# Second block's attention: the division of the probabilities moved from VectorE to GpSimd

## The chip, the cores and the metric

The kernel runs on one core of one Trainium2 chip. The metric is the device time of one execution in microseconds (us). One core has five engines, each with its own instruction stream: TensorE (PE in the profile, with PEld for its weight loads), VectorE (DVE), ScalarE (ACT), GpSimd (POOL) and SyncE (SP), which here issues the weight transfers. Engines wait for each other by semaphores only.

## What is computed

Two transformer-like blocks of two layers each over 256 tokens of width 1024, all in 32-bit floats. The first block is not touched. Of the second block each layer is attention with 16 softmax maps and then 16 experts of which each picks 32 tokens:

```
s = jnp.einsum(...).astype(jnp.float32) * scale          # 256 x 256 per head
s = s + bias        # 4 neighbourhood heads; 6 latent heads have no bias; 6 window heads have a mask and a sink logit
p = jax.nn.softmax(s, axis=-1).astype(v.dtype)
o = einsum(p, v)
h = h + concat(rms_norm(o_a), rms_norm(o_b), rms_norm(o_c)) @ w_out[l]
h = h + expert_choice_ffn(rms_norm(h, ffn_norm[l]), w_router[l], w_gate[l], w_up[l], w_down[l])
```

## The kernel before

Every engine's program is written out by hand in one order, and no scheduler changes it. In the second block the order of the attention part of a layer is the list `window_order(l)`: all engines walk the same list, and each executes of a step what is its own. I call this stretch of a layer "the window"; in the profile it lies at about 1060 to 1122 us (layer 0) and 1636 to 1700 us (layer 1). A map is called a unit, numbered 0 to 15: units 0 to 3 have a bias, 4 to 9 are the latent heads, 10 to 15 have the mask and the sink. A unit s goes through these steps:

- `s_qk` (TensorE): the scores, 128x512 (128 queries a partition, two halves of them, 256 keys each) into a PSUM bank.
- `m_max` (VectorE): adds the bias where there is one (L1654), takes the maximum (L1662), with the sink a maximum with it, and writes its negative (L1650, 128x2), signal `nmax`.
- `e_exp` (ScalarE): two exponentials 128x256 with their sums (L2443), with the sink one more of 128x2; signal `exp2`. It writes one of four buffers `sc2[2 + s % 4]`, and so waits for the transposes of unit s - 4.
- `n_norm` (VectorE): for sink units adds the sink's term to the sums (L1646, 128x2), the reciprocal of the sums (L1666, 128x2), and two multiplications in place, one for each half of 128x256 (L1650); signal `scaled2`.
- `t_turn` (TensorE): four transposes (L707, for units 0 to 3 L711), `c_copy` (ScalarE) their copy from PSUM (L2447), `v_pv` (TensorE) the product with the values for a pair of units, `w_out` (ScalarE) its square and its scaled copy, `q_stat` (TensorE) sums of the squares, `o_w` (TensorE) the output projection of a group of heads, `y_x` (VectorE, L1654 into x) its addition to the residual.

The three output groups g have a root each (`r_root`): VectorE sums (L1662) and scales (L1650), GpSimd raises to the power -1/2 (L2968), and VectorE waits for that. Before the window, `l_mkv` copies and `l_rot` rotates on VectorE. Some steps have idle matmuls put ahead of them (`SPARE`), which fill a wait of TensorE.

The experts' weights are fetched by SP in one fixed queue. The first of them for a layer go into room that the window frees: blocks "combine" wait for `v_pv` 4, "rest" for `s_qk` 15, "more" for `t_turn` 15, the next ones for `v_pv` 7 and one for the router. Every engine's helpers have `own()`, a wait for the engine's own last instruction. GpSimd's whole program in the second block before the change is the roots.

Of the kernel before, what the change touches and what calls it, by code (L numbers as in the profile page):

```python
# [17 lines left out]
def const_arrays():  # L18
# [65 lines left out]
    "merge": "gate gate_t bra brb mA gated merged gt1 gt1_dg gt2 gt2_dg",  # L84
    "hidden": "relu relu2 h1_hi h1",
    "latent": "lat_sq latent cro nab aqk cqT mq mkv mq_rot acT mT",
    "attn2": "s2 biased nmax exp2 scaled2 pT2 pv2 sq2 oT2",
    "group": "stat g_sum xg",
    "route": "router logits aff_e aff affT chosen sel slot Pm0 Pm xn xs0 xs1 PA PW x_apart",
    "norm": "root normed",  # L90
# [210 lines left out]
def program(nc, a, c1off, c2off, out):  # L301
    ctx = ExitStack()
    with ctx:
# [397 lines left out]
        def tensor(e):  # L701
# [697 lines left out]
                    psum.until(psum.at["s2", l, s], A, "exp2", l, s)  # L1399

            def t_turn(l, s):
                e.wait_ge(*V("scaled2", l, s))
                k, pb = bank("pT2", l, s)
                e3 = v4(sc2[2 + s % 4], 2)
                for t in range(2):
                    for kt in range(2):
                        turn_ = tr_flipped if s < 4 else tr
                        m = turn_(pb[:, 256 * t + 128 * kt:256 * t + 128 * kt + 128], e3[:, t, 128 * kt:128 * kt + 128])
                m.then_inc(*P.up("pT2", l, s))
# [228 lines left out]
        def vector(e):  # L1638
# [29 lines left out]
            def step():  # L1668
                return V.up("step")
# [631 lines left out]
            def n_norm(l, s):  # L2301
                u, st = units[s], S(f"u{s}", 10)
                e.wait_ge(*A("exp2", l, s))
                if u["sink"] is not None:
                    tt(st[:, 4:6], st[:, 4:6], st[:, 8:10], ALU.add).then_inc(*step())
                reciprocal(st[:, 6:8], st[:, 4:6]).then_inc(*step())
                e3 = v4(sc2[2 + s % 4], 2)
                for t in range(2):
                    m = ts(e3[:, t, :], e3[:, t, :], st[:, 6 + t:7 + t], None, ALU.mult)
                    m.then_inc(*(V.up("scaled2", l, s) if t else step()))  # L2310

            def r_root(l, g):
                c0, nc = groups[g]
# [645 lines left out]
        def pool(e):  # L2959

            def own():
                if G.last is not None:
                    e.wait_ge(*G.last)

            def root(v, *key):
                e.wait_ge(*V("root", *key))
                own()
                e.tensor_tensor(v, v, bc(K("nhalf"), [128, v.shape[1]]), ALU.pow).then_inc(*G.up("root", *key))  # L2968

            def levels(l):  # L2970
                e.wait_ge(*V("LT", l, 1))
                for s in range(1, 6):
                    for i in range(2):
                        if s > 1:
                            e.wait_ge(*P("B", l, s - 1, i))
                        a8, l8 = (z[:, i].rearrange("p t h c -> p (t h) c") for z in (AT, LT))
                        own()
                        e.tensor_tensor(a8, l8, bc(K(("lvF" if i == 0 else "lvB") + str(s)).unsqueeze(1), [128, 8, 64]),
                                        ALU.mult).then_inc(*G.up("AT", l, s, i))

            root(rstd[:, :], "x0", 0)
            for l in range(2):
                root(S("ya_ss", 8), "ya", l)
                levels(l)
                root(S("yb_ss", 8), "yb", l)
                root(rstd[:, :], "out", l)
                root(rstd[:, :], "mlp", l)
            for l in range(2):
                root(S("lat", 4), "lat", l)
                for g in range(3):  # L2990
                    root(S(f"gss{g}", 2), "g", l, g)
                root(rstd[:, :], "out2", l)
                if l == 0:
                    root(rstd[:, :], "moe", l)
            for t in range(2):
                root(rstd[:, t:t + 1], "last", t)
# [107 lines left out]
```

## Time and profile before

| | |
|---|---|
| median of 3 runs | 2171.55 us (2168.85 to 2175.55) |
| the profiled execution's own time, its span | 2170.66 us, 2169.4 us |
| busy: PE, DVE, ACT, POOL | 1861.0, 905.7, 643.6, 43.2 us |
| DMA, mean over the span | 285 GB/s |
| window of layer 0, 1060 to 1122 us: PE, DVE, ACT, POOL busy | 58.12, 51.51, 37.06, 1.39 us |
| window of layer 1, 1636 to 1698 us: the same | 54.27, 51.39, 37.24, 1.39 us |

A row of a timeline has its start, its length, the engine, the line, the operation, output <- input, and in brackets the idle time of the engine before it with what ended that. Rows of one kind that follow each other are merged (x8 is eight instructions). A multiplication of four passes stands as several MATMUL rows. Matmul lengths are modelled at their ends, so two rows may overlap a little. `ar`, `small`, `c`, `ring`, `x` are memory areas of the program, `pb` a PSUM bank.

### The profile page before, as it was taken

The page shows a single profiled execution, that of the slowest core. Times are in us where ns is not written, and L with a number is a line of the kernel's source. Part 1 is how long each engine was busy: PE and PEld are TensorE (multiplying, and loading weights), DVE is VectorE, ACT ScalarE, POOL GpSimd, SP SyncE. Part 2 cuts the span into 40 slices and gives each one's busy share as a digit, 9 for nine tenths or more (in the row PEclk, how much of TensorE's full clock was granted, in tenths as well). Part 3 has the DMA queues.
Part 4 walks back from the last instruction along what each step waited for, and adds up shares of the span by engine and source line. Part 5 has one row for each costly group of instructions (what it writes and reads, how often), then busy time and mean ns, then how long its engine had stood idle before and what let it go on. Part 6 is the DMA issues. An engine that isn't in the chain of part 4 may idle for free.

```text
span 2169.4 us, 31018 instructions
## 1 busy us (share of the span) xinstructions
PE 1861.0 (86%) x12840; PEld 1233.1 (57%) x12840; DVE 905.7 (42%) x1506; ACT 643.6 (30%) x1110; POOL 43.2 (2%) x46
## 2 busy tenths in 40 slices
PE   6999999999999999999898866676798997666666
PEld 3887888987888888988754311121275542121212
DVE  3675585655576576645762200000058520000002
ACT  3244235545244235534452100000055410000001
POOL 0001000000001000000000000000000000000000
PEclk8999999999999999999999987888899998888888
DMA  9565348456634344553749999999984799999997
GB/s 339 217 233 195 118 155 311 178 184 221 233 117 157 118 156 157 193 194 83 258 193 374 428 426 428 426 428 426 422 264 160 310 408 427 426 427 427 427 425 315
DMA packets 119749, 617.45 MB, mean 285 GB/s; under 512 B 18448, under 2 KB 21434, under 8 KB 86586
## 3 DMA queue, kind: packets, MB, share of 16 engines
q1 hardware_dynamic: 119034, 613.85, 71.6%
q8 instruction: 102, 1.67, 0.3%
q10 hardware_dynamic: 576, 1.63, 0.2%
q14 instruction: 37, 0.30, 0.0%
HBM read 614.40 MB, written 1.05 MB: 284 GB/s over the span
## 4 chain that ended last, share of the span: by engine, by line
PE 59%; DMA 27%; DVE 9%; ACT 2%; issue 1%; SPq 0%; POOL 0%; DVEq 0%; ACTq 0%
PE pb L704 57%; DMA ring<-in_w_up_dram 18%; DMA ar<-in_w_up_dram 4%; DMA x<-in_w_up_dram 3%; PE pb L707 2%; DVE ar L1654 2%; DVE ar L1646 1%; ACT ar L2443 1%; DMA ring<-in_ada_w_dram 1%; DMA ring<-in_w_down_dram 1%; DVE ar L1650 1%; DVE small L1662 1%; DVE x L1646 1%; ACT ar L2447 0%; DVE ar L1658 0%
## 5 line engine op out<-in xcount | busy, mean ns | idle before, releaser
L704 PE MATMUL pb<-ring,ar 128*32 128x512 f32 (+2 forms) x2144 | 408.5, 731 | 183.1 <-DMA ring<-in_w_up_dram 102.5
L704 PE MATMUL pb<-ar 64*64 64x64 f32 (+10 forms) x3680 | 418.9, 348 | 37.8 <-DMA ring<-in_w_up_dram 30.8
L2447 ACT COPY ar<-pb 128x512 f32<-128x512 f32 (+2 forms) x195 | 112.7, 578 | 910.1 <-PE pb L704 852.3
L1658 DVE COPY ar<-pb 128x512 f32<-128x512 f32 (+3 forms) x94 | 57.5, 612 | 723.2 <-PE pb L704 713.5
L704 PEld LDWEIGHTS pb<-ring,ar 128*32 128x32 f32 (+1 forms) x2144 | 106.4, 133 | 397.0 <-issue 383.0
L704 PEld LDWEIGHTS pb<-ar 64*64 64x64 f32 (+5 forms) x3680 | 217.9, 146 | 188.9 <-issue 165.9
L704 PE MATMUL pb<-hT,ring 128*128 128x256 f32 x1024 | 235.4, 386 | 0.4 <-ACT ar L2443 0.4
L704 PEld LDWEIGHTS pb<-hT,ring 128*128 128x128 f32 x1024 | 193.0, 192 | 33.6 <-issue 7.8
L1646 DVE TENSOR_TENSOR ws<-ring,ws 128x1024 fp32r<-128x1024 f32 x128 | 156.9, 1226 | 123.8 <-ACT ws L2447 122.0
L704 PE MATMUL pb<-hs,ws 128*128 128x256 f32 x1536 | 186.0, 283 | 3.7 <-ACT aux L2447 1.5
L704 PEld LDWEIGHTS pb<-hs,ws 128*128 128x128 f32 x1536 | 184.7, 192 | 5.6 <-ACT aux L2447 1.7
L704 PE MATMUL pb<-ws,h1s 128*128 128x512 f32 x768 | 175.7, 390 | 0.0
L2447 ACT CAST ws<-ring 128x1024 fp32r<-128x1024 f32 x128 | 134.2, 1048 | 127.2 <-PE pb L704 123.4
L704 PEld LDWEIGHTS pb<-ws,h1s 128*128 128x128 f32 x768 | 144.0, 188 | 30.8 <-issue 1.0
L704 PE MATMUL pb<-wp,hp 128*128 128x512 f32 (+1 forms) x636 | 140.0, 380 | 3.3 <-DVE wp L1646 1.6
L704 PEld LDWEIGHTS pb<-wp,hp 128*128 128x128 f32 x636 | 114.7, 190 | 27.3 <-DVE wp L1646 3.9
L707 PE MATMUL pb<-c,ar 128*128 128x128 f32 (+3 forms) x580 | 85.8, 283 | 23.8 <-DMA c<-in_c_dram 9.2
L707 PEld LDWEIGHTS pb<-c,ar 128*128 128x128 f32 (+3 forms) x580 | 68.7, 155 | 65.9 <-issue 39.9
L704 PE MATMUL pb<-hT,ar 128*32 128x512 f32 x200 | 67.2, 805 | 34.3 <-DMA ring<-in_w_up_dram 34.3
L1646 DVE TENSOR_TENSOR wp<-ring,wp 128x1024 fp32r<-128x1024 f32 (+1 forms) x53 | 61.2, 1155 | 55.9 <-ACT wp L2447 54.4
L2447 ACT CAST wp<-ring 128x1024 fp32r<-128x1024 f32 (+1 forms) x53 | 52.6, 992 | 56.0 <-PE pb L704 54.9
L1654 DVE SCALAR_TENSOR_TENSOR ar<-ar,pb 128x256 f32<-128x256 f32 (+1 forms) x84 | 40.7, 485 | 64.8 <-ACT ar L2443 57.7
(177 smaller groups left out, 1647.8 us busy)
## 6 DMA issues: line engine op xcount, KB each, us to landing
ring<-in_w_down_dram SPq DMA_DIRECT2D x46, 2048.0 KB, 28.1
ring<-in_w_gate_dram SPq DMA_DIRECT2D x42, 2048.0 KB, 28.4
ring<-in_w_up_dram SPq DMA_DIRECT2D x42, 2048.0 KB, 23.6
ring<-in_w_mlp_dram SPq DMA_DIRECT2D x32, 2048.0 KB, 7.9
ring<-in_w_in_dram SPq DMA_DIRECT2D x27, 2048.0 KB, 9.2
ring<-in_ada_w_dram SPq DMA_DIRECT2D x24, 2048.0 KB, 8.0
ar<-in_w_gate_dram SPq DMA_DIRECT2D x12, 2048.0 KB, 27.7
ar<-in_w_up_dram SPq DMA_DIRECT2D x12, 2048.0 KB, 23.5
```

The source lines that it names most:

```text
L704: return e.matmul(o, l, r, start=start, stop=stop)
L707: return e.transpose(o, i, ident[0:i.shape[0], 0:i.shape[0]])
L1646: return e.tensor_tensor(o, i0, i1, op)
L1650: return e.tensor_scalar(o, i, s1, s2, op0, op1)
L1654: return e.scalar_tensor_tensor(out=o, in0=i0, scalar=s, in1=i1, op0=op0, op1=op1)
L1658: return e.tensor_copy(o, i)
L1662: return e.tensor_reduce(o, i, AX.X, op)
L2443: return e.activation(o, i, fn, scale=scale, **kw)
L2447: return e.copy(o, i)
```

## The change

Of `n_norm` VectorE keeps the sink's addition and the reciprocal, whose signal is now `whole2`. The two multiplications of 128x256 go to GpSimd, which waits for `whole2` and, ahead of each, for its own last instruction; TensorE's `t_turn` now waits for GpSimd's signal. GpSimd walks `window_order` for these and for the three roots, so a root now stands behind the divisions that the list has ahead of it.

```diff
--- before.py
+++ after.py
@@ -84,7 +84,7 @@
     "merge": "gate gate_t bra brb mA gated merged gt1 gt1_dg gt2 gt2_dg",
     "hidden": "relu relu2 h1_hi h1",
     "latent": "lat_sq latent cro nab aqk cqT mq mkv mq_rot acT mT",
-    "attn2": "s2 biased nmax exp2 scaled2 pT2 pv2 sq2 oT2",
+    "attn2": "s2 biased nmax exp2 whole2 scaled2 pT2 pv2 sq2 oT2",
     "group": "stat g_sum xg",
     "route": "router logits aff_e aff affT chosen sel slot Pm0 Pm xn xs0 xs1 PA PW x_apart",
     "norm": "root normed",
@@ -1399,7 +1399,7 @@
                     psum.until(psum.at["s2", l, s], A, "exp2", l, s)
 
             def t_turn(l, s):
-                e.wait_ge(*V("scaled2", l, s))
+                e.wait_ge(*G("scaled2", l, s))
                 k, pb = bank("pT2", l, s)
                 e3 = v4(sc2[2 + s % 4], 2)
                 for t in range(2):
@@ -2303,11 +2303,7 @@
                 e.wait_ge(*A("exp2", l, s))
                 if u["sink"] is not None:
                     tt(st[:, 4:6], st[:, 4:6], st[:, 8:10], ALU.add).then_inc(*step())
-                reciprocal(st[:, 6:8], st[:, 4:6]).then_inc(*step())
-                e3 = v4(sc2[2 + s % 4], 2)
-                for t in range(2):
-                    m = ts(e3[:, t, :], e3[:, t, :], st[:, 6 + t:7 + t], None, ALU.mult)
-                    m.then_inc(*(V.up("scaled2", l, s) if t else step()))
+                reciprocal(st[:, 6:8], st[:, 4:6]).then_inc(*V.up("whole2", l, s))
 
             def r_root(l, g):
                 c0, nc = groups[g]
@@ -2978,6 +2974,17 @@
                         e.tensor_tensor(a8, l8, bc(K(("lvF" if i == 0 else "lvB") + str(s)).unsqueeze(1), [128, 8, 64]),
                                         ALU.mult).then_inc(*G.up("AT", l, s, i))
 
+            def n_norm(l, s):
+                e3 = v4(sc2[2 + s % 4], 2)
+                e.wait_ge(*V("whole2", l, s))
+                for t in range(2):
+                    own()
+                    m = e.tensor_scalar(e3[:, t, :], e3[:, t, :], S(f"u{s}", 10)[:, 6 + t:7 + t], None, ALU.mult)
+                    m.then_inc(*(G.up("scaled2", l, s) if t else G.up("step")))
+
+            def r_root(l, g):
+                root(S(f"gss{g}", 2), "g", l, g)
+
             root(rstd[:, :], "x0", 0)
             for l in range(2):
                 root(S("ya_ss", 8), "ya", l)
@@ -2987,8 +2994,9 @@
                 root(rstd[:, :], "mlp", l)
             for l in range(2):
                 root(S("lat", 4), "lat", l)
-                for g in range(3):
-                    root(S(f"gss{g}", 2), "g", l, g)
+                for step_, *key in window_order(l):
+                    if step_ in ("n_norm", "r_root"):
+                        (n_norm if step_ == "n_norm" else r_root)(l, *key)
                 root(rstd[:, :], "out2", l)
                 if l == 0:
                     root(rstd[:, :], "moe", l)
```

The order of VectorE's instructions changes in 16 places of each layer in the same way. The first piece is VectorE in layer 0, from the division of unit 2 to that of unit 6, with the maximum of unit 7 between (`pb6` and so on are the PSUM banks). Before:

```order
L1666 RECIPROCAL small<-small 128x2
L1650 TENSOR_SCALAR ar<-ar,small 128x256 x2
L1666 RECIPROCAL small<-small 128x2
L1650 TENSOR_SCALAR ar<-ar,small 128x256 x2
L1666 RECIPROCAL small<-small 128x2
L1650 TENSOR_SCALAR ar<-ar,small 128x256 x2
L1662 TENSOR_REDUCE small<-pb6 128x2
L1650 TENSOR_SCALAR small<-small 128x2
L1666 RECIPROCAL small<-small 128x2
L1650 TENSOR_SCALAR ar<-ar,small 128x256 x2
```

And now, the same stretch and the maxima of units 8 and 9 behind it:

```order
L1666 RECIPROCAL small<-small 128x2 x3
L1662 TENSOR_REDUCE small<-pb6 128x2
L1650 TENSOR_SCALAR small<-small 128x2
L1666 RECIPROCAL small<-small 128x2 x2
L1662 TENSOR_REDUCE small<-pb7 128x2
L1650 TENSOR_SCALAR small<-small 128x2
L1662 TENSOR_REDUCE small<-pb1 128x2
L1650 TENSOR_SCALAR small<-small 128x2
```

What moved: the multiplications are gone, and the maxima stand directly behind the reciprocals. The second piece is VectorE at the end of layer 0's window: the divisions of units 13 and 14, an addition to x, the maximum of unit 15, another addition to x, the division of unit 15. Before:

```order
L1650 TENSOR_SCALAR ar<-ar,small 128x256 x2
L1654 SCALAR_TENSOR_TENSOR x<-pb0,small,x 128x512
L1654 SCALAR_TENSOR_TENSOR ar<-pb2,ar 128x512
L1662 TENSOR_REDUCE small<-ar 128x2
L1650 TENSOR_SCALAR small<-small,sinks 128x2
L1650 TENSOR_SCALAR small<-small 128x2
L1654 SCALAR_TENSOR_TENSOR x<-pb3,small,x 128x512
L1646 TENSOR_TENSOR small<-small 128x2
L1666 RECIPROCAL small<-small 128x2
L1650 TENSOR_SCALAR ar<-ar,small 128x256 x2
```

And now:

```order
L1646 TENSOR_TENSOR small<-small 128x2
L1666 RECIPROCAL small<-small 128x2
L1654 SCALAR_TENSOR_TENSOR x<-pb0,small,x 128x512
L1654 SCALAR_TENSOR_TENSOR ar<-pb2,ar 128x512
L1662 TENSOR_REDUCE small<-ar 128x2
L1650 TENSOR_SCALAR small<-small,sinks 128x2
L1650 TENSOR_SCALAR small<-small 128x2
L1654 SCALAR_TENSOR_TENSOR x<-pb3,small,x 128x512
L1646 TENSOR_TENSOR small<-small 128x2
L1666 RECIPROCAL small<-small 128x2
```

Here too only the multiplications went. The third piece is GpSimd in one layer of the second block, from the latent part's root to the root of the last group. Before:

```order
L2968 TENSOR_TENSOR small<-small,c 128x4
L2968 TENSOR_TENSOR small<-small,c 128x2 x3
L2968 TENSOR_TENSOR rstd<-rstd,c 128x2 x2
```

And now:

```order
L2964 TENSOR_TENSOR small<-small,c 128x4
L2982 TENSOR_SCALAR ar<-ar,small 128x256 x16
L2964 TENSOR_TENSOR small<-small,c 128x2
L2982 TENSOR_SCALAR ar<-ar,small 128x256 x10
L2964 TENSOR_TENSOR small<-small,c 128x2
L2982 TENSOR_SCALAR ar<-ar,small 128x256 x6
L2964 TENSOR_TENSOR small<-small,c 128x2
L2964 TENSOR_TENSOR rstd<-rstd,c 128x2 x2
```

The divisions of units 0 to 7 stand ahead of the first group's root, those of 8 to 12 ahead of the second's, those of 13 to 15 ahead of the third's.

## Rows read from the trace of the kernel before

**Rows 1.** The page's second part: DMA share and rate in 40 slices.
```profile
DMA  9565348456634344553749999999984799999997
GB/s 339 217 233 195 118 155 311 178 184 221 233 117 157 118 156 157 193 194 83 258 193 374 428 426 428 426 428 426 422 264 160 310 408 427 426 427 427 427 425 315
```
**Rows 2.** The chain that ended last, in order of time: start, length, what.
```profile
1226.70 24.17 DMA ar<-in_w_up_dram
```
**Rows 3.** Busy time in three stretches, both windows and a short one behind.
```profile
1060.00:1122.00 62.00, 58.12 (x298) 38.34 (x298) 51.51 (x138) 37.06 (x100) 1.39 (x2) 0.96 0.44 170
...
1636.00:1698.00 62.00, 54.27 (x286) 34.45 (x284) 51.39 (x136) 37.24 (x103) 1.39 (x2) 1.00 0.44 170
...
1156.00:1160.00 4.00, 4.00 (x38) 1.87 (x31) 1.70 (x2) 0.00 (x0) 0.00 (x0) 1.00 0.25 57
```
**Rows 4.** Timeline of SP, layer 0: two of its issues.
```profile
1122.76 0.33 SPq L3051 DMA_DIRECT2D ar<-in_w_up_dram  x1
...
1158.92 0.33 SPq L3051 DMA_DIRECT2D ring<-in_w_gate_dram  x1
```
**Rows 5.** Groups of VectorE from 1060 to 1122 us, shapes apart.
```profile
L1650 DVE TENSOR_SCALAR ar<-ar,small 128x256 f32<-128x256 f32 x32 | 11.3, 353 | 1.1
...
L1666 DVE RECIPROCAL small<-small 128x2 f32<-128x2 f32 x16 | 2.7, 166 | 1.9 <-POOL small L2968 0.8
```
**Rows 6.** GpSimd: its largest group (ns min/median/max); timeline rows, one of VectorE.
```profile
L2978 POOL TENSOR_TENSOR ar<-ar,c x20: 1090/1092/1601, 199.6 to 712.4; 128x512 f32<-128x512 f32 x20
...
207.33 2.33 POOL L2978 TENSOR_TENSOR ar<-ar,c 128x512 f32<-128x512 f32 x2 [4.68 <-PE pb L704]
...
1094.44 0.17 DVE L1650 TENSOR_SCALAR small<-small 128x2 f32<-128x2 f32 x1
...
1094.69 0.70 POOL L2968 TENSOR_TENSOR small<-small,c 128x2 f32<-128x2 f32 x1 [42.67 <-DVE small L1650]
```
**Rows 7.** Timeline from 199 us, GpSimd and VectorE working at once.
```profile
199.56 3.10 POOL L2978 TENSOR_TENSOR ar<-ar,c 128x512 f32<-128x512 f32 x2 [26.21 <-DVE ar L1646]
200.24 1.46 DVE L1646 TENSOR_TENSOR ar<-c,ar 128x512 f32<-128x512 f32 x1
...
203.24 0.69 DVE L1646 TENSOR_TENSOR ar<-c,ar 128x512 f32<-128x512 f32 x1
```
**Rows 8.** Timeline of TensorE, layer 0: transposes of units 5, 7, 11+12, 13+14, 15.
```profile
1088.09 0.66 PE L707 MATMUL pb<-c,ar 128*128 128x128 f32 x4 [1.15 <-DVE ar L1650]
...
1092.18 0.66 PE L707 MATMUL pb<-c,ar 128*128 128x128 f32 x4 [0.30 <-DVE ar L1650]
...
1108.23 1.40 PE L707 MATMUL pb<-c,ar 128*128 128x128 f32 x8
...
1116.17 1.04 PE L707 MATMUL pb<-c,ar 128*128 128x128 f32 x8
...
1122.08 0.66 PE L707 MATMUL pb<-c,ar 128*128 128x128 f32 x4 [0.83 <-DVE ar L1650]
```
**Rows 9.** Timelines of ScalarE, then VectorE, layer 0.
```profile
1086.48 1.95 ACT L2447 COPY ar<-pb 128x512 f32<-128x512 f32 x3
...
1090.16 0.47 ACT L2443 ACTIVATE ar<-pb,small 128x256 f32<-128x256 f32 x1 [0.46 <-DVE small L1650]
...
1119.29 0.51 ACT L2443 ACTIVATE ar<-ar,small 128x256 f32<-128x256 f32 x1 [1.16 <-DVE small L1650]
...
1121.28 0.74 DVE L1650 TENSOR_SCALAR ar<-ar,small 128x256 f32<-128x256 f32 x2
```
**Rows 10.** Timeline of TensorE, layer 1: units 4, 8, 13 and 14, 15.
```profile
1662.92 0.66 PE L707 MATMUL pb<-c,ar 128*128 128x128 f32 x4 [0.43 <-DVE ar L1650]
...
1675.78 0.66 PE L707 MATMUL pb<-c,ar 128*128 128x128 f32 x4 [0.72 <-DVE ar L1650]
...
1696.27 1.39 PE L707 MATMUL pb<-c,ar 128*128 128x128 f32 x8
...
1698.25 0.66 PE L707 MATMUL pb<-c,ar 128*128 128x128 f32 x4 [0.24 <-DVE ar L1650]
```

## The prediction

> **What bounds the kernel now.** I read four views in this order. First the page's slices: in the experts' part of both layers of the second block the DMA engines move 426 to 428 GB/s without a gap, and between these parts they don't [rows 1]. The chain that ended last says the same: behind 1226 us it is landings of expert weights, some 24 us each, with a few of TensorE's products between them [rows 2]. So the experts' part ends a fixed time after its stream has begun to run without holes, and the window counts through the moment at which it lets the stream go. Then the issues of SP: those that wait for the window are released one by one, "more" at 1122.76 by `t_turn` 15, and after more of TensorE's work one stands at 1158.92, the last before which the DMA engines stood mostly still, with a share of 0.25 from 1156 to 1160 us [rows 3, 4]. From there on nothing waits. A window that ends earlier by d moves all of these by d, and the kernel's end too; each layer pays by itself.
>
> Next, what bounds the window. By busy time VectorE looks like it: 51.5 us of 62, and 12.5 us of that belong to the change. But TensorE is busy for 58.1 us of the 62 in layer 0 and 54.3 in layer 1 [rows 3]. So I looked for the places where TensorE really waits for a division. In layer 0 there are four: 1.15 us at unit 5, 0.30 at unit 7, 0.83 at unit 15, and one hidden in a row: the transposes of units 11 and 12 take 1.40 us for eight, where eight in a row elsewhere take 1.04, so 0.36 of waiting for unit 12 [rows 8]. Together 2.64 us. In layer 1 they are 0.43, 0.72, 0.24 and 1.39 - 1.04 = 0.35, together 1.74 us [rows 10]. What VectorE is freed of elsewhere shortens nothing: TensorE has other work there.
>
> **The change part by part.** Removed from VectorE: per unit two multiplications of 353 ns [rows 5], in a pair 0.74 us [rows 9], with the gap behind it 0.78; 16 units, 12.5 us per layer. The reciprocal of 166 ns stays.
>
> Added to GpSimd: 32 multiplications of 128x256 per layer by a scalar per partition. The trace has none. The nearest row is GpSimd's product of two tensors of 128x512, 1.09 us [rows 6]. With half the elements and one tensor read I take half of it, 0.55 us; below, it can't well beat VectorE's 0.35; above, the full row's 1.09 (all of its cost fixed). Between the two of a pair stands the wait for the own last instruction: two products of 1.09 take 2.33, so 0.15 us of gap [rows 6]. A pair is 1.25 us (0.85 to 2.35). The hand-over from VectorE is small: its instruction ends at 1094.61 and GpSimd's begins at 1094.69, 0.08 us [rows 6]. So a division that follows its exponential at once is ready 0.08 + 1.25 = 1.33 us after the reciprocal instead of 0.76: 0.57 later. One that stood in VectorE's queue is ready earlier.
>
> The Trainium skill, "GPSIMD Engine Reference", section 4.1, says that elementwise work belongs on VectorE, GpSimd being about 2 times slower for two inputs and roughly at line rate for one. By line rate at its 1.2 GHz an instruction would be an estimated 0.21 us and a fixed part, and the gain some tenths larger than below; no run here shows it yet.
>
> Layer 0, in order. Units 0 and 1 have other work of TensorE's ahead of their transposes. Up to 1088.4 us ScalarE works without a pause worth naming (three copies from 1086.48 end it) [rows 9], so the exponentials 3 to 7 don't come earlier whatever VectorE does, and what units 2, 3, 4 gain is not used. Unit 5 is ready about 1.0 us earlier, but the product behind it needs the second of ScalarE's three copies, which ends at 1087.8, and what follows needs the exponential of unit 8, for which ScalarE idles 0.46 us now [rows 9]. That idle goes, and nothing more: of the first two waits (1.45 us) 0.5 comes through. The wait of 0.36 goes wholly, since VectorE then has the maximum of unit 13 and the division of unit 12 done microseconds early. Last the 0.83 at unit 15. Now the exponential of 15 starts at 1119.29 after ScalarE idled 1.16 for its maximum, so its work was done at 1118.13; the multiplications start 2.0 us after it, at 1121.28 [rows 9]. With VectorE ahead it starts as soon as ScalarE is free, at 1118.13 - 0.86 = 1117.3; 2.0 for exponentials, addition and reciprocal and 1.33 for GpSimd give 1120.6. TensorE would be free at 1121.25 - 0.86 = 1120.4, so 0.2 to 0.3 of waiting stays. Layer 0: 0.5 + 0.36 + 0.83 - 0.3 = 1.4 us.
>
> Layer 1. Units 0 and 1 have no cover: their transposes follow their division at once, and come 0.1 and 0.5 us late, of which 0.1 reaches ScalarE's unbroken work behind it. Of the 0.43 at unit 4 the copy ahead of the next product leaves 0.3. Unit 8 waits 0.72 now; its maximum's predecessor comes 0.5 earlier and GpSimd takes 0.57 more, so nothing at that place, but the exponentials behind keep the 0.5. At units 13 to 15 0.35 + 0.24 go, and 0.2 stay as GpSimd's length. With 0.3 for a PSUM bank that unit 15's maximum frees late now: -0.1 + 0.3 + 0.5 + 0.59 - 0.2 + 0.3 - 0.2 (ScalarE) = 1.2 us.
>
> The three roots wait behind divisions that are done by then (the first is wanted at 1094.7, and unit 7's transposes start at 1092.2 [rows 6, 8]): nothing. GpSimd's four buffers, SP's queue and the DMA work stay as they are.
>
> Contention. When GpSimd and VectorE both worked on two tensors in SBUF, VectorE's product took 1.46 us instead of 0.69, and GpSimd's first pair 3.10 instead of 2.33 [rows 6, 7]. In the windows VectorE's long instructions read PSUM or one tensor, and the 128x2 ones are 28 per layer. If each that meets a running multiplication (GpSimd is busy 18 of 60 us) waits half of it, that is 28 x 0.3 x 0.28 = 2.4 us of VectorE per layer, nearly all in time it has just been given: I take 0.1 per layer on the path, 0 to 0.6 as bounds.
>
> The Trainium skill, "SBUF — State Buffer", section "Who interferes with whom", says that VectorE's two-input instructions and its two-port modes (copies and scalar operations from SBUF to SBUF) lock GpSimd out for their whole length, and the other way round. By that rule the trace agrees with the rows of the pair above, and the small scalar operations of `m_max` would be met as well.
>
> Sum: 1.4 + 1.2 - 0.2 = 2.4 us. Against the profiled execution's 2170.66 us (span 2169.4) that gives 2168.3; the median of the runs is 0.9 above that execution, so I say 2169.2. The smallest change that a measurement of this kernel can tell from none is about 0.3%, 6.5 us.
>
> **The rivals.**
> - *GpSimd is the new bound (slower).* In layer 0 the divisions of units 2 to 6 follow each other at the pace of ScalarE's exponentials, about the 1.25 us of a pair. A longer pair queues up: at 2.35 us it falls behind by 1.1 a unit, 5.5 us over five, of which I take 1.4 as covered, 4.1; 1.2 us of waits later in the window go, 1.0 is added at unit 15: +3.9. In layer 1 unit 4 is late by 1.3, +1.5 at the end. Sum +5.4: 2177, still inside 0.3%. It turns from gain to loss at about 0.8 us an instruction, and is slower by over 0.3% from 1.2 us on. At 2 us an instruction GpSimd's 32 would take 66 us, more than a window, and each layer some 12 us: 2195. For it: no row has the operation, its scalar is fetched from memory, and the smallest root takes 0.70 us for 2 elements [rows 6] (it is a power, so I don't price by it). Chance 0.15 for over +6.5 us, 0.15 for a loss within it.
> - *VectorE is the bound after all (faster).* Its rows have no idle time in the windows, and if each wait of ScalarE and TensorE were in the end its fault, all of TensorE's idle time could go: 2.6 us in layer 0, 62 - 54.3 = 7.7 in layer 1, together 10 us, of which GpSimd's latency leaves perhaps 7: 2164.5. Against it: ScalarE's unbroken work [rows 9] and a TensorE that is already nearly full. Chance 0.08 (half of it over 6.5 us).
> - *Blocked ports.* By the mechanism of rows 7 the maxima ahead of units 8 and 15 lose 0.6 each: a gain of 1.2 less, 2170.4. That is the rule of the skill's page named above, were it to apply to the 128x2 instructions. Chance 0.12.
> - *The stream doesn't care.* If the hole at 1158.92 is set by something other than TensorE's order, the windows end earlier and the kernel does not: 2171.5. Against it: that issue waits for TensorE. Chance 0.05.
>
> **How the numbers follow.** My forecast, 1 to 4 us faster, 0.45; the rest as above. Within 0.3%: 0.45 + 0.15 + 0.04 + 0.12 + 0.05 = 0.81, of which I give 0.02 to the faster side for what I may have read too small; faster 0.06, same 0.79, slower 0.15. The range goes down to the rival with 7 us of gain, 2164.5, and up to the bound of GpSimd's price, 2177.5; it leaves out the 0.15 above and a few hundredths below.
>
> **What would show it.** GpSimd's group of 32 x 2 multiplications: at 0.45 to 0.65 us I am right in the price. VectorE's busy time in each window falls from 51.5 to 40. TensorE's waits at units 5, 7, 12 of layer 0 are gone, that at 15 is 0.2 to 0.3 and now put down to GpSimd. SP's issue at 1158.92 comes 1.4 us earlier. VectorE's small instructions beyond 170 ns would show the ports. I am wrong if an instruction of GpSimd takes over 0.8 us, or if TensorE's start of the window's end moves and the last issue does not.

## The result and the profile after

The changed kernel takes 2188.80 us in the median of four runs (2188.32 to 2192.54), the kernel before 2173.09 on the same chip. The ratio is 1.0073, 95% interval [1.0057, 1.0088]: 0.7% slower, about 15.7 us. The forecast was 2169.2, its range ended at 2177.5: the time lies outside it. The profiled execution took 2189.19 us, its span is 2187.8 (before 2169.4), 18.4 us more.

First GpSimd's largest group by line and shape in the changed kernel, over the whole span (busy us, mean ns, idle time before it and what ended it):

```profile
L2982 POOL TENSOR_SCALAR ar<-ar,small 128x256 f32<-128x256 f32 x64 | 59.3, 926 | 79.5 <-DVE small L1666 73.5 <-POOL ar L2982 2.2 <-DVE small L1650 0.7
```

An instruction takes 926 ns, not 550. GpSimd's timeline in layer 0, where the divisions of units 2 to 7 come one after another:

```profile
1083.63 1.94 POOL L2982 TENSOR_SCALAR ar<-ar,small 128x256 f32<-128x256 f32 x2 [4.22 <-DVE small L1666]
...
1087.85 1.94 POOL L2982 TENSOR_SCALAR ar<-ar,small 128x256 f32<-128x256 f32 x2 [0.17 <-POOL ar L2982]
...
1094.17 1.94 POOL L2982 TENSOR_SCALAR ar<-ar,small 128x256 f32<-128x256 f32 x2 [0.17 <-POOL ar L2982]
```

A division is done every 2.11 us. VectorE's timeline shows when the reciprocals ahead of them are done, those of units 2, 3 and 4 in one row of three, then units 6 and 7:

```profile
1083.37 0.70 DVE L1666 RECIPROCAL small<-small 128x2 f32<-128x2 f32 x3 [0.46 <-DVE small L1650]
...
1087.52 0.17 DVE L1666 RECIPROCAL small<-small 128x2 f32<-128x2 f32 x1 [1.32 <-ACT ar L2439]
...
1092.48 0.17 DVE L1666 RECIPROCAL small<-small 128x2 f32<-128x2 f32 x1 [2.66 <-ACT ar L2439]
```

So five units (2 to 6) arrive between 1083.5 and 1087.7, one in 1.04 us on average. TensorE wants them more slowly. In the kernel before it began the transposes of unit 2 at 1084.59, the row below, and those of unit 7 at 1092.18 [rows 8]: one unit in 1.52 us on average.

```profile
1084.59 0.60 PE L711 MATMUL pb<-ar 128*128 128x128 f32 x4
```

At 2.11 us a unit there is a queue. What TensorE makes of it, from its timeline in the changed kernel:

```profile
1087.74 0.66 PE L711 MATMUL pb<-ar 128*128 128x128 f32 x4 [0.59 <-POOL ar L2982]
1089.85 0.66 PE L707 MATMUL pb<-c,ar 128*128 128x128 f32 x4 [1.45 <-POOL ar L2982]
1091.95 1.12 PE L707 MATMUL pb<-c,ar 128*128 128x128 f32 x4 [1.45 <-POOL ar L2982]
1093.00 1.98 PE L704 MATMUL pb<-ar 128*64 128x256 f32 x8
...
1108.37 1.08 PE L704 MATMUL pb<-ar 128*64 128x256 f32 x8
...
1127.04 0.66 PE L707 MATMUL pb<-c,ar 128*128 128x128 f32 x4 [1.45 <-POOL ar L2982]
...
1127.90 4.52 PE L704 MATMUL pb<-ring,hT 128*128 128x512 f32 x6
```

Up to unit 7 one wait of 1.15 us and one of 0.30 stood [rows 8]. Now there are 0.59, 1.45 and 1.45 at units 3, 4 and 5 and one of 0.55 at unit 1 ahead of them (not shown), and later 1.45 at unit 14 where unit 15 had 0.83; the releaser is GpSimd each time. Then something that the prediction has no word on: four transposes take 1.12 us instead of 0.66, and the eight products at 1093.00 take 1.98 instead of the 1.08 that they take at 1108.37. Stretches of the changed kernel say why, first the whole windows of layer 0 and layer 1 (stretch, its length, busy time and count of the engines, granted clock, DMA share, GB/s):

```profile
1067.96:1134.05 66.09, 60.21 (x287) 37.77 (x286) 35.23 (x91) 35.77 (x97) 30.61 (x34) 0.87 0.41 160
1651.58:1717.54 65.96, 54.06 (x288) 33.87 (x288) 41.83 (x104) 37.26 (x102) 31.09 (x34) 1.00 0.41 160
...
1088.00:1092.00 4.00, 1.09 (x9) 0.62 (x7) 1.64 (x4) 2.01 (x6) 3.55 (x4) 0.81 0.00 0
1092.00:1096.00 4.00, 4.00 (x18) 2.54 (x18) 0.17 (x1) 3.02 (x9) 3.58 (x4) 0.50 0.00 0
...
1100.00:1104.00 4.00, 4.00 (x16) 2.13 (x18) 2.71 (x10) 0.54 (x2) 2.47 (x3) 0.50 0.00 0
1104.00:1108.00 4.00, 4.00 (x16) 1.82 (x12) 2.05 (x7) 3.57 (x11) 3.26 (x5) 0.98 0.02 4
1128.00:1132.00 4.00, 4.00 (x7) 1.52 (x6) 0.33 (x2) 1.86 (x6) 1.38 (x2) 0.57 0.07 30
1160.00:1164.00 4.00, 1.97 (x10) 1.72 (x10) 1.96 (x8) 0.77 (x1) 0.00 (x0) 0.77 0.65 190
1164.00:1168.00 4.00, 4.00 (x14) 3.46 (x15) 1.02 (x3) 0.00 (x0) 0.00 (x0) 0.50 0.88 369
```

The waits leave TensorE busy for 1.09 us of the 4 from 1088 on, and within them, about 1090.5, the granted clock goes to 0.50, 1.2 instead of 2.4 GHz (0.75 in the microsecond from 1090 on, 0.50 in the next). It is back at 1.00 soon after 1104, some 14 us later. For the last 12 of them TensorE never stops, and its rows take up to twice as long. A shorter fall follows the wait at 1127.04, and a third one comes behind the window, in the rows from 1160 and 1164. In layer 1's window the waits are there too, and the clock stays at 1.00. VectorE's busy time did fall about as the prediction said (by 11.5 us): over the window, bounded as below, from 45.8 to 35.2 us in layer 0 and from 51.3 to 41.8 in layer 1.

The stream follows the window. These are two issues of SP of the changed kernel, the ones of [rows 4] at 1122.76 and 1158.92:

```profile
1134.05 0.33 SPq L3059 DMA_DIRECT2D ar<-in_w_up_dram  x1
...
1173.27 0.33 SPq L3059 DMA_DIRECT2D ring<-in_w_gate_dram  x1
```

From here on I measure each layer's window by three issues of SP: the first of a w_up tile into the ring, the one that `t_turn` 15 releases, and the last one ahead of the unbroken stream. From the first to the second it is "the window", from the first to the third "the layer". Before, the window is 55.64 us and the layer 91.80 in layer 0 (from 1067.12), 62.01 and 99.38 in layer 1 (from 1636.92). Differences to that, in the profiled executions, beside the medians of all runs:

| kernel | median us | ratio to before, 95% interval | window, layer 0 | layer 0 | window, layer 1 | layer 1 |
|---|---|---|---|---|---|---|
| the change | 2188.80 | 1.0073 [1.0057, 1.0088] | +10.45 | +13.51 | +3.95 | +4.07 |
| e1 one product | 2173.44 | 1.0000 [0.9989, 1.0010] | -1.16 | +0.44 | -0.60 | -0.39 |
| e2 no division | 2172.53 | 0.9995 [0.9984, 1.0006] | -1.53 | -1.31 | -1.34 | -0.93 |
| e3 filled waits | 2181.41 | 1.0037 [1.0024, 1.0050] | +4.56 | +4.77 | +4.81 | +5.87 |
| e4 units 8 to 12 | 2175.16 | 1.0008 [0.9999, 1.0016] | +0.26 | +0.30 | +5.36 | +5.35 |
| e5 layer 0 only | 2184.00 | 1.0042 [1.0027, 1.0057] | +10.37 | +10.36 | 0.00 | 0.00 |
| e6 unused products | 2182.68 | 1.0034 [1.0024, 1.0045] | +2.62 | +4.22 | +6.43 | +6.64 |
| e7 two products | 2192.02 | 1.0075 [1.0058, 1.0093] | +8.60 | +8.81 | +6.68 | +8.47 |
| e8 where covered | 2173.17 | 0.9996 [0.9984, 1.0007] | -1.47 | -1.27 | +0.01 | +1.59 |
| e9 unused single | 2197.67 | 1.0112 [1.0099, 1.0126] | +12.71 | +14.29 | +10.47 | +10.67 |
| e10 halves | 2172.66 | 1.0002 [0.9994, 1.0011] | -1.08 | +0.51 | -0.39 | -0.40 |
| e11 layer 1 only | 2178.07 | 1.0023 [1.0012, 1.0034] | -0.03 | +3.08 | +3.87 | +3.86 |
| e12 covered and filled | 2173.27 | 1.0003 [0.9994, 1.0012] | -1.47 | -0.70 | -0.21 | +0.56 |

One of e7's six runs (3605.95 us) and one of the 24 of the kernel before beside it (3612.05) were slow and are left out here and below.

In the changed kernel 13.51 + 4.07 and 0.84 ahead of the first window make the 18.4 us of the span; between the layers it has 0.3 us more and behind them 0.3 less. The stretch ahead of the first window, which the change doesn't touch, differs by -1.4 to +2.9 us between these executions; the medians of before, 2173.1 to 2173.7, lie 2.4 to 3.0 above its own profiled execution. So a single trace is good for differences of a layer and not for the whole to a microsecond.

### The profile page after: what moved, and what is told of

It is laid out like the page before. It is cut to its first block, busy times and chain, and to the rows that moved or that the text cites. A ratio compares the mean times of both kernels' runs of the same rounds, so it can differ in the third digit from the quotient of the medians.

```text
span 2187.8 us, 31050 instructions
## 1 busy us (share of the span) xinstructions
PE 1872.8 (86%) x12840; PEld 1241.5 (57%) x12840; DVE 884.2 (40%) x1442; ACT 643.9 (29%) x1110; POOL 102.6 (5%) x110
## 4 chain that ended last, share of the span: by engine, by line
PE 60%; DMA 27%; DVE 7%; ACT 2%; POOL 1%; issue 1%; SPq 0%; DVEq 0%; ACTq 0%; POOLq 0%
PE pb L704 57%; DMA ring<-in_w_up_dram 17%; DMA ar<-in_w_up_dram 4%; PE pb L707 2%; DMA ring<-in_w_down_dram 2%; DMA x<-in_w_up_dram 2%; DVE ar L1654 1%; POOL ar L2982 1%; DVE ar L1646 1%; DMA ring<-in_ada_w_dram 1%; ACT ar L2439 1%; DVE small L1662 1%; DVE x L1646 1%; DVE ar L1658 0%; ACT ar L2443 0%
## 5 line engine op out<-in xcount | busy, mean ns | idle before, releaser
L704 PE MATMUL pb<-ar 64*64 64x64 f32 (+10 forms) x3680 | 423.3, 351 | 34.0 <-DMA ring<-in_w_up_dram 28.6
L2964 POOL TENSOR_TENSOR rstd<-rstd,c 128x2 f32<-128x2 f32 (+1 forms) x10 | 6.7, 668 | 1430.6 <-DVE rstd L1650 1430.6
```

Source lines behind the costliest of these rows:

```text
L704: return e.matmul(o, l, r, start=start, stop=stop)
```

## The experiments

Three questions: is it GpSimd's time per unit, what is TensorE's clock worth, and does GpSimd disturb VectorE?

**One product instead of two multiplications (e1).** The price alone is changed. GpSimd's product of two tensors is given the reciprocals broadcast along the row:

```
-                for t in range(2):
-                    own()
-                    m = e.tensor_scalar(e3[:, t, :], e3[:, t, :], S(f"u{s}", 10)[:, 6 + t:7 + t], None, ALU.mult)
-                    m.then_inc(*(G.up("scaled2", l, s) if t else G.up("step")))
+                own()
+                e.tensor_tensor(e3, e3, bc(S(f"u{s}", 10)[:, 6:8].unsqueeze(2), [128, 2, 256]), ALU.mult).then_inc(*G.up("scaled2", l, s))
```

> GpSimd divides a unit by one product of two tensors over 128x512 (the reciprocals broadcast) in place of two multiplications of 128x256. Theory P (price): the loss is only that two multiplications take 1.94 us a unit and queue at 2.11 us, while ScalarE delivers a unit each 1.25 us or so. The product should take 1.1 to 1.2 us, the price that the forecast had, and the kernel should come out 0 to 4 us faster than before (2169 to 2173 us). Theory C (contention): GpSimd and VectorE block each other; a product reads two tensors and blocks more, so the kernel stays at least 6 us slower than before (over 2179). Theory M (map): the forecast misread which waits of the window count, and even at its own price it loses, 3 us or more.

2173.44 us, ratio 1.0000. The whole loss is gone with nothing changed but the form of GpSimd's work. Its group by line and shape:

```profile
L2981 POOL TENSOR_TENSOR ar<-ar,small 128x512 f32<-128x512 f32 x32 | 33.3, 1041 | 88.7 <-DVE small L1666 87.4
```

Five divisions in a row in GpSimd's timeline:

```profile
1085.64 5.78 POOL L2981 TENSOR_TENSOR ar<-ar,small 128x512 f32<-128x512 f32 x5 [5.11 <-DVE small L1666]
```

A unit takes 1.04 us in one instruction and 1.94 in two of half the size. Five take 5.78, 1.16 each with the gaps, less than the 1.52 at which TensorE takes them. Of its waits in layer 0's window for a division two are left, 0.49 at unit 5 and 0.22 at unit 15.

**No division at all (e2).** The multiplications are left out on both engines, so the output is made of undivided probabilities; `t_turn` waits for the reciprocal.

> The multiplications are left out altogether, on both engines; the probabilities go on undivided (VectorE still makes the reciprocals, and the transposes wait for them). This is what freeing VectorE is worth with no latency of GpSimd at all. Theory P: the forecast's walk without its 1.25 us pair, 3 to 5 us faster than before (2168 to 2170). Rival (VectorE is the bound of the window after all): 7 to 15 us faster (2158 to 2166). Theory M: another value, above all none at all.

2172.53 us, 0.9995. The windows are 1.53 and 1.34 us shorter, and that is all that 22 us less busy time of VectorE (905.7 to 883.4) is worth.

**Waits filled (e3).** GpSimd divides as in the change. TensorE makes products that nobody reads ahead of four transposes of layer 0, so that it works while it waits:

```
+SPARE.update({("t_turn", 3): (1, 0), ("t_turn", 4): (3, 0), ("t_turn", 5): (3, 0), ("t_turn", 14): (3, 0)})
```

> The changed kernel with idle matmuls of TensorE ahead of the transposes of units 3, 4, 5 and 14 of layer 0 (1, 3, 3 and 3 of them, 0.43 us each at full clock), where it waits for GpSimd 0.59, 1.45, 1.45 and 1.45 us. Theory K (clock): about half of the loss of layer 0 is that TensorE's granted clock falls to 0.5 behind these waits; filled, it stays at 1.0, the stretch from 1092 to 1104 us takes some 5 us less, and the kernel is 5 to 8 us faster than the changed one (2181 to 2184). Rival: the waits alone are the loss, the clock only a sign of them, and the kernel stays within 2 us of the changed one (2187 to 2191).

2181.41 us, 7.4 less than the change. TensorE's timeline of this kernel at the place where the clock fell:

```profile
1089.68 0.66 PE L710 MATMUL pb<-c,ar 128*128 128x128 f32 x4
1090.18 1.46 PE L707 MATMUL pb<-c 128*128 128x256 f32 x6
1091.79 0.66 PE L710 MATMUL pb<-c,ar 128*128 128x128 f32 x4 [0.15 <-POOL ar L2985]
1092.37 1.08 PE L707 MATMUL pb<-ar 128*64 128x256 f32 x8
```

And the window there, with the granted clock as the third number from the end:

```profile
1092.00:1096.00 4.00, 3.52 (x29) 2.30 (x27) 0.18 (x2) 3.44 (x10) 3.59 (x4) 1.00 0.01 4
```

GpSimd is as late as before, but TensorE has worked in the meantime, the clock stays at 1.00, and the transposes and products are back at 0.66 and 1.08. The window of layer 0 is 5.9 us shorter than the change's. What is left, 4.56, is what the late divisions cost at full clock. Layer 1, untouched here, came 0.9 us later in its window and 1.8 in the layer than in the change: its granted clock fell in this execution (0.83 from 1655 to 1665, 0.59 from 1708 to 1712), which it did not in the change's window.

**GpSimd only where the queue is short (e4).** Units 8 to 12 go to GpSimd in both layers, the others stay on VectorE:

```
+                on_pool = 8 <= s < 13
+                reciprocal(st[:, 6:8], st[:, 4:6]).then_inc(*(V.up("whole2", l, s) if on_pool else step()))
+                if not on_pool:
...
+                        m = ts(e3[:, t, :], e3[:, t, :], st[:, 6 + t:7 + t], None, ALU.mult)
...
```

> GpSimd divides only units 8 to 12 of both layers, VectorE the others. In the changed kernel's layer 0 TensorE never waits for these five; in layer 1 it waits for 8 (1.98 us) and 9 (0.44). Theory P: layer 0 loses nothing and gains some tenths, layer 1 loses 1 to 1.5 us at unit 8: between 1 us faster and 2 us slower than before (2172 to 2175). Theory C: contention costs wherever GpSimd works, 10 of its 32 divisions, so a third of the loss, 5 us.

2175.16 us, 1.0008. Layer 0 loses 0.3 us, layer 1 5.4, all of it at one place of TensorE's timeline; the third line is a stretch of 10 us with its granted clock (from 1678 to 1688 it is 0.50 throughout):

```profile
1676.35 0.65 PE L707 MATMUL pb<-c,ar 128*128 128x128 f32 x4 [1.99 <-POOL ar L2990]
...
1679.50 2.08 PE L704 MATMUL pb<-ar 64*128 64x256 f32 x8
...
1680.00:1690.00 10.00, 10.00 (x42) 5.76 (x38) 2.72 (x9) 3.35 (x9) 4.19 (x5) 0.59 0.19 47
```

The wait at unit 8 of layer 1, 0.72 us before [rows 10], is 1.99, and what follows runs at half the clock. One wait that is 1.3 us longer costs 5.4 here. But the change has the same wait at the same place, behind the same products of 3.60 us, and the eight products that took 2.08 take 1.13, with a granted clock of 1.00:

```profile
1692.87 0.66 PE L707 MATMUL pb<-c,ar 128*128 128x128 f32 x4 [1.98 <-POOL ar L2982]
...
1695.57 1.13 PE L704 MATMUL pb<-ar 64*128 64x256 f32 x8
...
1696.00:1700.00 4.00, 4.00 (x33) 2.57 (x30) 2.10 (x6) 2.04 (x7) 1.77 (x3) 1.00 0.00 0
```

The traces of e7 (2.16) and e11 (1.97) have no fall behind this wait either. So a wait of this length can be followed by a fall of the clock and needn't be; what decides it, these runs don't show. Nor do the times say how often e4 has it: its median is only 1.5 above before's, but its fastest of eleven runs (2174.54) is 4.7 above the fastest of before (2169.80).

**The layers apart (e5, e11).** The same switch with `l == 0` and with `l == 1`.

> GpSimd makes the divisions of layer 0 alone; in layer 1 they are VectorE's again. If each layer pays by itself: layer 0's stream is late by the 13.5 us of the changed kernel and layer 1 by nothing, 2187.5 us less the change's 4.1 us of layer 1, so some 2173.7 + 14.3 - 0.8 = 2187, and GpSimd's instructions are again 0.93 us. If the layers lose alike (half of the 15 us each): about 2181. If the loss of layer 0 were an accident of that one execution, anything from 2177 to 2183.

> GpSimd makes the divisions of layer 1 alone. If each layer pays by itself, and the 4.1 us by which layer 1's stream was later in the changed kernel are all of it: 2177 to 2179, and together with layer 0 alone (2184.0, 10.2 above before) the sum of both is 14 to 15, the change's. If layer 1's loss hangs on layer 0's (buffers, clock): 2174.

2184.00 and 2178.07 us, 10.3 and 4.8 above the kernel before that ran beside them. Together 15.1, the change's 15.7 within the intervals: the layers pay each for itself. The expectation for layer 0 alone was 3 us too high, as it took the third fall of the clock in the change's trace, behind the window, for a part of the loss. It isn't there in e5 (10.37 in the window, 10.36 in the layer), and it is there in layer 0 of e11, where the program is that of before. Two rows of TensorE's timeline in e11, the second at half the clock (the same six products took 1.54 in other executions):

```profile
1150.88 0.29 PE L707 MATMUL pb<-c,ar 16*128 16x16 f32 x2 [1.74 <-DVE ar L2344]
...
1152.76 2.91 PE L704 MATMUL pb<-c 128*128 128x256 f32 x6
```

That fall makes a layer 1.6 or 3.1 us later (e1, e6, e8, e9 and e10 have it in one layer by 1.6, e7 by 1.8, e11 and the change by 3.1), whatever divides. In some layers the clock falls at another place behind the window and costs next to nothing (e4, layer 0). The traces of before, e5 and e12 have no fall behind a window, which for before goes with its medians being above its trace.

**Two products (e7).** Each unit gets the cheap form of e1, but with a copy of it ahead, into a buffer that nobody reads (`for to in (q3, e3)`, of which only the second product writes `e3`).

> Each unit's division on GpSimd is one product of two tensors, 128x512, the form that cost nothing when it stood alone, but with a copy of it ahead that goes into a buffer nobody reads: a unit takes 2 x 1.04 + 0.15 = 2.23 us and comes every 2.3 to 2.4 us, against 1.95 and 2.11 in the changed kernel. If it is only GpSimd's time per unit that counts, this is as slow as the change or slower: 2188 to 2196, again with TensorE's waits on GpSimd at units 5 to 8 and a granted clock of 0.5 behind them. If the operation with a scalar per partition has a harm of its own, this stays near 2174 to 2178.

2192.02 us, 1.0075. GpSimd's timeline has twelve in a row without a gap, six units of 2.28 us each:

```profile
1084.59 13.66 POOL L2984 TENSOR_TENSOR ar<-ar,small 128x512 f32<-128x512 f32 x12 [4.51 <-DVE small L1667]
```

So a slow division costs as much without the multiplication by a scalar, and no harm of its own is needed to explain the change. At 1.16 us a unit it costs nothing, at 2.11 15.7 us, at 2.28 18.3 (2192.02 against 2173.69 beside it). The last two can't be told apart: their intervals overlap, and in the traces e7 loses less than the change in layer 0 (8.60 in the window against 10.45), with the clock at 0.50 for a shorter time, some 7 us against 17, and more in layer 1. Nor is e7 clean: VectorE's 128x2 instructions take up to 1.03 us beside its products.

**Work that nobody waits for (e6, e9).** VectorE divides as before, and GpSimd makes what it makes in the change, for units 0 to 12, but of constants, and into a buffer that nobody reads. In e9 it makes one product of 128x512 instead.

```
+                e3 = v4(spare_buf[:, 0:512], 2)
...
+                    m = e.tensor_scalar(e3[:, t, :], c1[:, 0:256], S(f"u{s}", 10)[:, 6 + t:7 + t], None, ALU.mult)
```

> VectorE divides as in the kernel before, and GpSimd makes multiplications of the same shape at the same places for units 0 to 12, of constants, into a buffer that nobody reads; TensorE waits for VectorE alone. If the loss is that TensorE waits for a late division: no change, 2173.7 within 0.3%, and TensorE has no wait on GpSimd. If GpSimd's instructions block VectorE's two-port operations in SBUF: VectorE's 128x256 multiplications go from 353 ns towards 1.2 us where they meet, the windows get longer by several us, 2180 or more. If they are slow because VectorE is in the way, they stay at 0.93 or get longer here.

> As with the unused products (VectorE divides, GpSimd works into a buffer nobody reads, units 0 to 12), but GpSimd makes one product of two tensors of 128x512 a unit, 1.04 us, instead of two with a scalar of 0.97. GpSimd's queue then keeps up, so the roots start when they are asked for (VectorE waits 0.81 us for each, not 1.70 and 2.87). If the 9 us of the unused products came from roots queued behind GpSimd's work and the clock that fell then: within 3 us of before, 2172 to 2176. If they came from both engines working in SBUF at once (VectorE's pair at 0.84 us instead of 0.74), most of it stays, since GpSimd meets as many pairs: 13 pairs a layer by 0.1, and what TensorE's clock adds, 2178 to 2183.

2182.68 and 2197.67 us. My theory said "no change" for e6: it fell, and I had to find a second effect. Three rows from VectorE's timeline in e6, two of layer 0 and one of layer 1:

```profile
1086.88 0.84 DVE L1651 TENSOR_SCALAR ar<-ar,small 128x256 f32<-128x256 f32 x2
...
1099.69 0.17 DVE L1667 RECIPROCAL small<-small 128x2 f32<-128x2 f32 x1 [1.70 <-POOL small L2969]
...
1680.12 0.69 DVE L1655 SCALAR_TENSOR_TENSOR ar<-pb,ar 128x512 f32<-128x512 f32 x1 [2.87 <-POOL small L2969]
```

Two things. VectorE's pair of multiplications takes 0.84 us beside GpSimd's (up to 0.97) instead of 0.74, and GpSimd's pair up to 2.22 instead of 1.94. And GpSimd's queue holds up the roots of r_root: VectorE waits 1.70 and 2.87 us for them instead of 0.81, in layer 1 TensorE then waits 2.56 at unit 8, and the clock falls. I took the second for the cause and expected e9 to be cheap, since one product keeps up. The roots are in time there (0.81), and the kernel is 24 us slower. From e9's timelines, VectorE's:

```profile
1086.76 1.62 DVE L1651 TENSOR_SCALAR ar<-ar,small 128x256 f32<-128x256 f32 x2
```

And GpSimd's:

```profile
1086.80 1.04 POOL L2988 TENSOR_TENSOR ar<-c,small 128x512 f32<-128x512 f32 x1 [6.42 <-DVE small L1667]
```

VectorE's pair takes 1.62 us instead of 0.74, in every unit from 0 to 12 (13 to 15, where GpSimd has no product, keep 0.74), while GpSimd's product keeps its 1.04. The 0.88 all fall on the first of the pair, 1.23 instead of 0.35. So beside GpSimd's product of two tensors VectorE's scalar multiplication stands for most of the product's length, and beside GpSimd's scalar multiplications hardly. In e6 both effects are there, and how its 9 us divide between them wasn't measured. In the changed kernel VectorE has no such multiplications left: its longest 128x2 instruction takes 0.38 us and the roots wait 0.84, once 1.16. Neither effect is its loss.

The Trainium skill, "SBUF — State Buffer", section "Who interferes with whom", says that whichever of the two engines is second on the shared ports blocks until the first is done. The trace of e9 agrees that one of the two stands (1.62 for 0.74), but by the recorded starts it is the first: VectorE's row begins at 1086.76, GpSimd's at 1086.80. The trace of e6 doesn't agree: overlapping scalar instructions cost VectorE's pair 0.1 to 0.23 us and GpSimd's up to 0.28.

**In search of a gain (e10, e8, e12).** In e10 VectorE multiplies one half of each unit and GpSimd the other. In e8 GpSimd makes one product, only for units whose transposes have other work ahead: layer 0 without 3, 5 and 15, layer 1 units 9 to 12. In e12 six more unread products cover TensorE's wait of 1.74 us behind the window, `("chosen",): (11, 11)` for `(5, 5)`, on top of e8.

> Each division is shared: VectorE multiplies the second half and GpSimd the first, side by side, and TensorE waits for both. A unit costs GpSimd 0.93 us and is ready about 1.0 us after the reciprocal instead of 0.76 on VectorE; GpSimd's queue keeps up with ScalarE's pace of 1.25 us. If the pace of the queue is what costs in the changed kernel: within 2 us of before, 2172 to 2176, with waits of TensorE on GpSimd of up to 0.5 us. If it is the mere latency of GpSimd, or both engines at work in SBUF: 2177 to 2183.

> GpSimd divides by one product of 128x512 (1.04 us), only for the units whose transposes have other work ahead of them: in layer 0 all but 3, 5 and 15, in layer 1 units 9 to 12; VectorE does the rest. The most that a freed VectorE gave was 1.3 us in layer 0 and 0.9 in layer 1 (multiplications left out). If TensorE's waits are what counts, this gives 0.5 to 2 us: 2172 to 2173.5, less than can be told from no change. If VectorE were the bound, 5 us or more: below 2169. If mixing the two engines makes one wait for the other in new places: 2175 to 2178.

> The kernel in which GpSimd divides only covered units by one product (2173.17), with eleven products of TensorE's that nobody reads instead of five ahead of its wait of 1.74 us for the chosen experts, in both layers. In half of the traces, of whatever kernel, the granted clock falls to 0.5 within the next microseconds (six products take 2.91 us instead of 1.54), which then makes that layer's stream 1.4 to 1.7 us later. If it is that wait that lets the clock fall: 1 to 2 us faster, 2171 to 2172.5, and no fall behind it in the trace. If the fall follows on something else: 2173, or later by what the six products add beyond the wait (nothing, they take 1.4 us).

2172.66, 2173.17 and 2173.27 us: all the same as before. e8 has the shorter window of e2 in layer 0 (-1.47) without leaving anything out, nothing in layer 1, and a fall of the clock gave the rest back in its trace. In e12 that fall is in neither layer (six products in 1.54), which one trace doesn't put down to the filling, since before and e5 have none either. And the eleven outlast the wait: from the wait for the affinities to the transposes behind it are 5.06 us instead of 4.29 (before: 1146.32 to 1150.61). The expected 1 to 2 us didn't come. No version beats the kernel before by what can be measured.

## Why the prediction was wrong

- **What bounds the kernel: right.** The stream moved with the window in every kernel, but for the falls of the clock behind it, and TensorE's waits, not VectorE's busy time, set the window. e2 gives the waits a worth of 1.53 and 1.34 us; before GpSimd's length was taken off, the working had 1.69 for layer 0 and some 1.4 for layer 1. The rival "VectorE is the bound after all" is out.
- **The price of GpSimd's multiplication: this step failed.** "With half the elements and one tensor read I take half of it, 0.55 us"; it is 0.926, over the 0.8 that the prediction itself named as the sign of being wrong. Half the elements didn't halve it, and a scalar from memory isn't cheaper than a second tensor: the full 128x512 product takes 1.04 in the same place (e1). The bound of 1.09 held, and so a pair of up to 2.35 against 1.94 measured. With one instruction of 1.04 a unit, less than the 1.25 that I took for a pair, the loss is gone: e1 is 2173.44. Of the 2.4 us of gain that the forecast had, its windows show 1.16 + 0.60 and its median nothing.
- **The rival that came true, "GpSimd is the new bound (slower)", was mis-sized.** Its place and its mechanism, a queue in units 2 to 6 of layer 0, are right, as e1, e3 and e7 show. Its pace of 1.25 us is not: that is ScalarE's two exponentials alone, and with the copies between them they start 1.43, 3.32 and 1.61 us apart in the trace of before (1083.80, 1085.23, 1088.55, 1090.16), while TensorE takes a unit every 1.52. It priced a pair of 2.35 us at +5.4 in all. The pair is 1.94, and the waits alone are +4.6 in layer 0 (e3) and +3.95 in layer 1 (window of the change at a clock of 1.00), 8.5 together. It had TensorE waiting at unit 4 of layer 1 (+1.5); in the trace unit 4 waits 0.17 us, and units 0, 1, 8, 14 and 15 between 0.68 and 1.98 each. In layer 0 it counted unit 1 as covered, which waits 0.55, and put the wait at the end at unit 15; it is 1.45 at unit 14.
- **The missing term: TensorE's granted clock.** Nothing in the prediction says that a wait can cost more than itself. In layer 0 the falls to 0.50 within the window cost 5.9 us (change against e3). With 8.5 that is 14.4, the sum of the two windows; 15.7 is measured. Whether the rest is the layer's tail, which falls now and then in all kernels, these runs don't separate.
- **Contention: right in size for this change** (0.2 taken, no long VectorE instruction shows), though for a reason that the prediction didn't have: the multiplications that GpSimd would have blocked had gone.
- **The range and chances.** The forecast stood on a median of three runs, 0.9 above the trace; the longer series lie 2.4 to 3.0 above it, so 2169.2 was some 2 us low before any of this. 2177.5 was the bound of the price with the clock left out. The 0.15 for a loss of over 0.3% needed 1.2 us an instruction in my sum; with the clock it came at 0.93.

The Trainium skill, "GPSIMD Engine Reference", section 4.1, has one-input work at roughly line rate, an estimated 0.21 us here. The trace disagrees: 0.926.

## What to carry to other kernels

Before work moves to another engine, compare its time per item there with the pace at which the next engine takes them: 1.16 us against 1.52 cost nothing, 2.11 cost 0.7% of a kernel though the engine was busy 5% of it. Price a wait of TensorE by what may follow it too: behind waits of 0.59, 1.45 and 1.45 us its clock was halved for 14 us, and a wait of 1.98 was followed by a fall in one trace and by none in another. If they can't be avoided, unread products in them are cheap, as long as they don't outlast them. And look for the form: one instruction over a whole unit, with the scalars broadcast, was twice as fast as two with a scalar each.

## What was unexpected of the hardware

- GpSimd: 128x256 by a scalar per partition 926 ns, 128x512 by a broadcast tensor 1041 ns. The broadcast costs nothing against a full second tensor (1092 before).
- TensorE: behind three waits, with 1.09 us of work in the 4 us around the last two, the granted clock was 0.50 for 14 us, the last 12 of them unbroken work; with the same divisions late but the waits filled, 1.00 throughout.
- VectorE's pair of 128x256 scalar multiplications beside GpSimd: 0.74 us alone, 0.84 to 0.97 beside its scalar multiplications, 1.62 beside its product of two tensors. Even an addition of 128x2 took 1.03 us beside such a product (e1, instead of 0.16).
- The fall of the clock behind the window comes in some traces and not in others where the program of that layer is the same (layer 0 of before and of e11), and is worth 1.6 or 3.1 us, as much as the gain that was looked for. The same holds within the window: the wait of 1.98 or 1.99 us at unit 8 of layer 1, with a fall in e4 (5.4 us) and none in the change.
